# The sample tokens of a state-space layer: layout changes through a DRAM scratch instead of TensorE transposes

## The chip, the cores and the metric

One core of a Trainium2 chip runs the whole kernel. The time is device microseconds of one execution, lower is better; of the kernel before the median of three runs is given.

## The reference

One layer of a streaming encoder runs on 1024 prompt tokens and 64 sample tokens (a second group of requests with state from the past). Both share the weights, so the kernel puts them side by side: 1088 columns.

```
h = rmsnorm(x); proj = h @ w_in                      # 2048 -> 6152 columns
u, z_ssm, q, k, v, z_att, f = split(proj)
# S5 branch: 64 groups of 16 channels, a complex diagonal state of 64 per group
bb = coef * (u_group @ B)                            # per token
h_t = abar * h_(t-1) + bb_t                          # scan over tokens, sample tokens start from a given state
y = real(C h) + D * u
y_ssm = rmsnorm(gelu(y) * sigmoid(gelu(y) @ w_glu + b) * silu(z_ssm))
# attention branch with forget gates: softmax(q k / sqrt(d) + c_t - c_s) v, * silu(z_att), rmsnorm
out = x + concat(y_ssm, y_att) @ w_out
```

## The kernel before

**The GEMM that runs through.** Every projection is a sum of pieces. A piece is 256 rows of a weight (`PIECE` 2 tiles of 128) for 128 output columns. SP loads it into one of four `wraw` slots (`Weights.load`), ScalarE rounds it to `whi` (`split_hi`, L169), VectorE takes the rest `wlo` (`split_lo`, L173), and TensorE multiplies it in 18 matmuls (`multiply`, L185: three products, two row tiles, three column groups of 384, 384 and 320) into the three banks of `GB`. A load waits for the split of the piece four before it, and a cast for the multiplication four before it. So a load is issued about eight pieces before its own multiplication.

**State-space passes.** The 1024 state-space channels are worked in 8 passes j of 128 channels (8 groups of 16). A pass has 16 piece steps s: s = 0 to 7 multiply the u columns of the pass after, s = 8 to 15 the z columns of this one; u of pass 0 comes ahead of the loop, and the last pass has only steps 8 to 15. All the other work of the pass hangs on these steps by the tables `FULL` and `LAST`: each engine has its own program, and at step s it first does its part of the piece and then the state-space step that the table puts there. The order of each engine is thus written out by hand. In `FULL`:

- `first`, before s = 0: eight transposes into LS (L1030), copied out by ScalarE (L483) and VectorE (L699).
- `st1` at 0: the 128 channels of u are turned for each of the L = 8 phases of a block of 8 tokens. For the prompt (L1054) a transpose gives 128 blocks x 128 channels, for the sample (L1055) 8 blocks x 128 channels. They are copied to UC and UCS.
- `k` at 1; `st2` at 2: UC and UCS are turned back by group (L1072, L1074), which gives Ug, rows (phase, channel) and columns (block), with one column for the state at `NB` and the 8 sample blocks behind it.
- `s` at 3, `scan` at 4, `back` at 5, `h` at 7: the states, with VectorE and GpSimd. `y` at 9: 16 matmuls (L1093, L1094), copied to Y by ScalarE and VectorE (L536, L754).
- `yt` at 10 and `z` at 12: the same two layout changes backwards for y (L1008 and L1009, then L1016 and L1018). ScalarE takes the gelu of both parts (L464, L466) into U and stores U to `zg_s` (L469), `z_act` is counted, and TensorE's next `first` waits for it.
- `fin` at 13: the final states are stored. At 15 ScalarE waits for the store of U and writes Silu of z into U (L495), which frees the banks of `GB`.
- GpSimd prepares the tables for the next pass after `h` (G at L905 to L910, TR at L922 to L929). VectorE prepares Q at steps 13 and 14 (`prepare_q`, L663 to L672).
- `toeplitz` at 12 on SP: eight DMAs from the scratch `kpad_s` into MT (L364), between weight loads.

The attention phase follows, in 8 heads of 32 piece steps. Its first head carries, on each engine but SP, the last steps of the last pass (`tail`).

## Time and profile before

| | us |
|---|---|
| median of three runs | 2100.68 (2100.58 to 2102.3) |
| the profiled execution | 2099.1 |
| its span | 2097.4 |
| PE busy | 2023.6 (96%) |
| DVE busy | 1029.0 (49%) |
| ACT busy | 709.4 (34%) |
| POOL busy | 481.3 (23%) |

The span runs from the first to the last instruction; the rest of the execution's time lies around it. PE is TensorE, PEld its weight loads, DVE VectorE, ACT ScalarE, POOL GpSimd; SPq and ACTq are the queues that issue DMAs. In a row `x8` counts instructions and the idle time stands in brackets or behind the last bar, with what ended it. Matmuls are pipelined: one lasts longer in the trace than the slot it takes, so slots are read from the chain of waits or from differences of starts.

### The profile page before, as it was taken

To read this page: it belongs to the slowest core of one execution; us is meant where nothing else is said; L and a number is where in the kernel's file an instruction comes from. 1 tells how busy PE (TensorE), PEld (TensorE's weight loads), DVE (VectorE), ACT (ScalarE), POOL (GpSimd) and SP (SyncE) were. 2 spreads that over 40 slices of the span, in tenths; PEclk is the share of its full clock that TensorE was granted. 3 is DMA by queue.
4 is the path that set the end of the run, shared out by engine and by line. 5 is a ranking of instruction groups with operands and counts; after the bars stand their busy time and mean duration, and the time that the engine had idled before them with its cause. 6 is when DMAs were issued, how large, how long until landed. Compare 5 with 4: busy or idle time off the path is not lost.

```text
span 2097.4 us, 36580 instructions
## 1 busy us (share of the span) xinstructions
PE 2023.6 (96%) x12880; PEld 1952.5 (93%) x12880; DVE 1029.0 (49%) x2028; ACT 709.4 (34%) x1460; POOL 481.3 (23%) x748
## 2 busy tenths in 40 slices
PE   4899999999999999999999999999998999999997
PEld 3689999999999999999999999999998999999997
DVE  6465465555545354554635455463565553333332
ACT  6423333233342333343343334334355631111110
POOL 5764455444411001010010101001020112222222
PEclk8899999999999999999999999999999999999998
DMA  7222222222222213122131212112174433333331
GB/s 204 81 49 61 64 68 58 61 72 63 69 61 57 60 33 85 35 59 55 34 82 33 83 35 73 41 43 73 36 264 149 156 122 94 85 85 85 85 85 55
DMA packets 194713, 162.16 MB, mean 77 GB/s; under 512 B 26690, under 2 KB 176364, under 8 KB 193316
## 3 DMA queue, kind: packets, MB, share of 16 engines
q1 hardware_dynamic: 174224, 98.87, 18.1%
q0 software_dynamic: 14832, 51.26, 8.0%
q10 hardware_dynamic: 5604, 11.34, 1.5%
q8 instruction: 31, 0.51, 0.1%
q14 instruction: 22, 0.18, 0.0%
HBM read 124.47 MB, written 36.95 MB: 77 GB/s over the span
## 4 chain that ended last, share of the span: by engine, by line
PE 90%; DVE 4%; ACT 2%; issue 2%; DMA 1%; POOL 0%; ACTq 0%; DVEq 0%; SPq 0%; POOLq 0%
PE GB L185 64%; PE TB L185 9%; PE TB L1870 3%; PE TB L1891 3%; PE TB L1912 1%; PE TB L1084 1%; PE TB L1093 1%; PE TB L1094 1%; PE TB L1971 1%; PE TB L1931 1%; DVE XL L597 1%; DVE xt L589 0%; PE TB L970 0%; PE TB L1054 0%; PE TB L1856 0%
## 5 line engine op out<-in xcount | busy, mean ns | idle before, releaser
L185 PE MATMUL GB<-XH,whi 128*128 128x384 f32 (+1 forms) x2880 | 973.7, 338 | 6.3 <-ACT QR L1425 3.8
L185 PE MATMUL GB<-XH,wlo 128*128 128x384 f32 (+1 forms) x2880 | 943.1, 327 | 0.0
L185 PE MATMUL GB<-XL,whi 128*128 128x384 f32 (+1 forms) x2880 | 940.0, 326 | 0.0
L173 DVE TENSOR_TENSOR wlo<-wraw,whi 128x256 fp32r<-128x256 f32 x544 | 259.8, 478 | 738.5 <-ACT whi L169 734.2
L185 PEld LDWEIGHTS GB<-XH,whi 128*128 128x128 f32 x2880 | 541.5, 188 | 20.8 <-issue 14.8
L185 PEld LDWEIGHTS GB<-XL,whi 128*128 128x128 f32 x2880 | 542.1, 188 | 5.3 <-issue 3.8
L169 ACT CAST whi<-wraw 128x256 fp32r<-128x256 f32 x544 | 220.0, 405 | 954.6 <-PE GB L185 801.0
L185 PEld LDWEIGHTS GB<-XH,wlo 128*128 128x128 f32 x2880 | 541.0, 188 | 0.0
L1291 POOL DMA_DIRECT2D ya_s<-ZR x7 | 4.1, 586 | 729.5 <-DVE ZR L1655 729.5
L1702 DVE RECIPROCAL SQ<-SQ 128x136 f32<-128x136 f32 x128 | 127.5, 996 | 1.1
L185 PE MATMUL TB<-XH,wlo 128*128 128x384 f32 (+1 forms) x384 | 125.8, 328 | 0.0
L185 PE MATMUL TB<-XH,whi 128*128 128x384 f32 (+1 forms) x384 | 125.5, 327 | 0.0
L185 PE MATMUL TB<-XL,whi 128*128 128x384 f32 (+1 forms) x384 | 125.5, 327 | 0.0
L1474 ACT ACTIVATE PR<-PR,nmx 128x128 f32<-128x128 f32 (+8 forms) x72 | 53.4, 742 | 186.2 <-DVE nmx L1673 173.0
L1379 ACT ACT_TABLE_LOAD x64 | 82.1, 1283 | 1.2
L1870 PE MATMUL TB<-PT,VT 128*128 128x128 f32 x576 | 74.7, 275 | 0.8 <-ACT PT L1484 0.8
L1870 PEld LDWEIGHTS TB<-PT,VT 128*128 128x128 f32 x576 | 71.3, 191 | 1.5 <-ACT PT L1484 1.2
L1891 PE MATMUL TB<-KN,QN 128*128 128x512 f32 (+2 forms) x192 | 72.4, 486 | 0.0
L185 PEld LDWEIGHTS TB<-XH,whi 128*128 128x128 f32 x384 | 72.1, 188 | 0.1
L185 PEld LDWEIGHTS TB<-XH,wlo 128*128 128x128 f32 x384 | 72.1, 188 | 0.0
L185 PEld LDWEIGHTS TB<-XL,whi 128*128 128x128 f32 x384 | 72.0, 188 | 0.0
L1668 DVE CUSTOM_DVE_ANT_0 PR<-TB,NCB 128x128 f32<-128x128 f32 (+3 forms) x64 | 41.0, 640 | 33.3 <-PE TB L1891 22.2
(387 smaller groups left out, 2197.2 us busy)
## 6 DMA issues: line engine op xcount, KB each, us to landing
wraw<-in_w_in SPq DMA_DIRECT2D x384, 128.0 KB, 2.2
wraw<-in_w_out SPq DMA_DIRECT2D x128, 128.0 KB, 2.2
xt<-in_x_prompt SPq DMA_DIRECT2D x5, 1024.0 KB, 5.4
NCB<-nc_s POOLq DMA_DIRECT2D x8, 608.0 KB, 5.3
zg_s<-U ACTq DMA_DIRECT2D x8, 544.0 KB, 2.7
XL<-zg_s SPq DMA_DIRECT2D x8, 544.0 KB, 4.4
VR<-zg_s POOLq DMA_DIRECT2D x8, 544.0 KB, 6.3
KO<-zs_s POOLq DMA_DIRECT2D x8, 544.0 KB, 7.7
```

The source lines that it names most:

```text
L169: S.copy(whi[:, s % SPL], wraw[:, s % RAW]).then_inc(self.hi, 1)
L173: V.tensor_tensor(wlo[:, s % SPL], wraw[:, s % RAW], whi[:, s % SPL].bitcast(f32), ALU.subtract).then_inc(self.lo, 1)
L185: ins = T.matmul(group(GB if bank is None else bank, b), w[:, s % SPL, kk], x[:, k + kk, c:c + n], start=first and kk == 0 and i == 0, sto ...
L597: V.tensor_tensor(XL[:, 4 * b:4 * b + 4, m * P:m * P + n], tb, XH[:, 4 * b:4 * b + 4, m * P:m * P + n].bitcast(f32), ALU.subtract).then_in ...
L1084: ins = T.matmul(TB[g * NP:(g + 1) * NP, c:c + SC], LS[:, i, g * NP:(g + 1) * NP], Ug[:, 2 * (i % 4) + g], start=True, stop=True)
L1093: T.matmul(TB[:, c:c + SC], MT[:, g], Ug[:, g], start=True, stop=False)
L1379: o.then(S.activation(tabs[:], epsc[:], func))
L1474: S.activation(PR[0:n, 0:w], PR[0:n, 0:w], ACT.Exp, bias=nmx[0:n], accum_out=rsum[0:n]).then_inc(e["exp"], 1)
L1668: V.tensor_tensor_reduce(out=PR[0:n, 0:w - n], in0=TB[0:n, 0:w - n], in1=NCB[0:n, c:c + w - n], scale=1.0, scalar=-3e38, op0=ALU.add, op1= ...
L1702: o.then(V.reciprocal(a, a))
L1870: ins = T.matmul(O, VT[:, b], PT[:, b * P:(b + 1) * P], start=b == 0, stop=b == i)
L1891: ins = T.matmul(TB[:, c:c + cw], q, KN[:, c:c + cw], start=True, stop=True)
```

## The change

Of the 64 sample tokens, u and y no longer go through narrow transposes. For u, ScalarE writes the sample columns of the bank to UST (in phase order), SP stores UST to the scratch `us_s` (128 x 64 floats) and loads it back in eight DMAs, one for each phase, into USG; VectorE copies USG to its columns of Ug. For y, VectorE gathers the sample columns of Y into YSG, SP stores it to `vs_s` and loads it back in eight DMAs, one for each group, into YST; ScalarE takes the gelu from there, now at the step `fin` (13) and ahead of the stores of the final states, with the store to `zg_s` behind it (`zs_step`). Each load moves runs of 8 floats, 128 of them. SP's order is: u out at the end of a pass, u in after the load of step 0, y out after step 2 and y in after step 3 of the following pass. Pass 0 and the first head of the attention phase are written out on SP, and the last y goes into that head. The L1055, L1009, L1074 and L1018 transposes and the four UCS copies (L457, L509, L686, L713) are gone. The signals `dec_ready` and `g_neg` are dropped or counted on others.

```diff
+    us_s = scratch("us_s", [P, DEC])
+    vs_s = scratch("vs_s", [P, DEC])
...
-            UCS = sbp("UCS", [P, 1024])
+            UCS = sbp("UCS", [P, 576])
+            UST, USG, YSG, YST = (sbp(n, [P, DEC]) for n in ("UST", "USG", "YSG", "YST"))
...
 
+                SIO = 16 * (1 + L)
+
+                def sample_u_out(j, taken):
+
+                    sp.wait_ge(e["ga"], taken)
+                    sp.wait_ge(e["us_io"], SIO * j)
+                    sp.dma_start(us_s, UST[:]).then_inc(e["us_io"], 16)
+
+                def sample_u_in(j):
+
+                    sp.wait_ge(e["us_io"], SIO * j + 16)
+                    sp.wait_ge(e["st2_dve"], j)
+                    for r in range(L):
+                        sp.dma_start(USG[r * GC:(r + 1) * GC].rearrange("c (g n) -> c g n", g=8),
+                                     us_s.rearrange("(g c) (t n) -> t c g n", g=8, t=L)[L - 1 - r]).then_inc(e["us_io"], 16)
+
+                def sample_y_out(j):
+
+                    sp.wait_ge(e["y_dve"], 2 * (j + 1))
+                    sp.wait_ge(e["vs_io"], SIO * j)
+                    sp.dma_start(vs_s, YSG[:]).then_inc(e["vs_io"], 16)
+
+                def sample_y_in(j):
+
+                    sp.wait_ge(e["vs_io"], SIO * j + 16)
+                    sp.wait_ge(e["z_act"], j)
+                    for g in range(8):
+                        sp.dma_start(YST[g * GC:(g + 1) * GC].rearrange("c (t n) -> c t n", t=L),
+                                     vs_s.rearrange("(t c) (g n) -> g c t n", t=L, g=8)[g]).then_inc(e["vs_io"], 16)
+
...
                 for s in range(HP):
                     W.load(sp, s, s, 0, PIECE * s)
-                with sp.Fori(0, NJ - 1) as j:
+                def pass_of(j, y):
                     for s in range(NPC):
                         load(j, s)
+                        if not y and s == HP - 1:
+                            sample_u_out(0, 3)
+                        if s == (0 if y else HP):
+                            sample_u_in(j)
+                        if y and s == 2:
+                            sample_y_out(j - 1)
+                        if y and s == 3:
+                            sample_y_in(j - 1)
                         if s == FULL["toep"]:
                             toeplitz(j)
+                    sample_u_out(j + 1, 5 * j + 5)
+                pass_of(0, False)
+                with sp.Fori(1, NJ - 1) as j:
+                    pass_of(j, True)
                 for s in range(HP, NPC):
                     load(NJ - 1, s)
+                    if s == HP:
+                        sample_u_in(NJ - 1)
+                    if s == HP + 2:
+                        sample_y_out(NJ - 2)
+                    if s == HP + 3:
+                        sample_y_in(NJ - 2)
                 toeplitz(NJ - 1)
+
+                def tail(s):
+                    if s == 8:
+                        sample_y_out(NJ - 1)
+                    if s == 9:
+                        sample_y_in(NJ - 1)
+                return tail
...
-                    S.copy(cols(UZ, 2), group(GB, 2)).then_inc(e["ga"], count)
+                    S.copy(UZ[:, 2 * CW:SEQ], GB[:, 1024:1024 + SEQ - 2 * CW])
+                    act.wait_ge(e["us_io"], 16 * (1 + L) * u)
+                    S.copy(UST[:].rearrange("p (t n) -> p t n", t=L),
+                           GB[:, 1024 + SEQ - 2 * CW:1024 + TOK - 2 * CW].rearrange("p (n t) -> p t n", t=L)).then_inc(e["ga"], count)
 
                 def yt_step(j):
                     act.wait_ge(e["yt_mm"], j + 1)
                     S.copy(UC[:].rearrange("p (t g c) -> p g t c", t=L, g=8)[:, 0:4],
-                           TB[:, 512:1024].rearrange("p (g t c) -> p g t c", g=4, t=L))
-                    S.copy(UCS[0:8].rearrange("p (t g c) -> p g t c", t=L, g=8)[:, 0:4],
-                           TB[0:8, 3 * 512:4 * 512].rearrange("p (g t c) -> p g t c", g=4, t=L)).then_inc(e["yt_act"], 1)
+                           TB[:, 512:1024].rearrange("p (g t c) -> p g t c", g=4, t=L)).then_inc(e["yt_act"], 1)
+
+                zt = lambda a: a.rearrange("p (c t) -> p t c", t=L)
 
                 def z_step(j):
                     act.wait_ge(e["z_mm"], j + 1)
-                    zt = lambda a: a.rearrange("p (c t) -> p t c", t=L)
                     for hlf in range(2):
                         S.activation(zt(U[:, 0:SEQ])[:, 4 * hlf:4 * hlf + 4],
                                      TB[:, 512 * (1 + hlf):512 * (2 + hlf)].rearrange("p (t c) -> p t c", t=4), ACT.Gelu)
-                    S.activation(zt(U[:, SEQ:TOK]), TB[:, 0:DEC].rearrange("p (t c) -> p t c", t=L),
+
+                def zs_step(j):
+                    act.wait_ge(e["vs_io"], 16 * (1 + L) * (j + 1))
+                    S.activation(zt(U[:, SEQ:TOK]), YST[:].rearrange("p (t c) -> p t c", t=L),
                                  ACT.Gelu).then_inc(e["z_act"], 1)
                     act.wait_ge(e["z_act"], j + 1)
                     act.dma_start(zg_s[ds(j * P, P), :], U[:, 0:TOK]).then_inc(e["zg_out"], 16)
...
                         if s == at["z"]:
                             z_step(j)
                         if s == at["fin"]:
+                            zs_step(j)
                             fin_step(j)
                 for s in range(HP):
...
+                        zs_step(NJ - 1)
                         fin_step(NJ - 1)
                 return tail
...
                         if s == at["st2"]:
                             dve.wait_ge(e["st2_mm"], j + 1)
                             dve.wait_ge(e["zs_out"], 16 * j)
                             V.memset(Ug[:, :, NB:NB + 1], 0.0)
                             V.tensor_copy(Ug[:, 4:8, 0:NB], TB[:, 3 * 512:4 * 512].rearrange("p (g c) -> p g c", g=4))
-                            V.tensor_copy(Ug[:, :, NB + 1:SC], TB[:, 4 * 512:4 * 512 + DEC].rearrange("p (g c) -> p g c", g=8)
+                            dve.wait_ge(e["us_io"], 16 * (1 + L) * (j + 1))
+                            V.tensor_copy(Ug[:, :, NB + 1:SC], USG[:].rearrange("p (g c) -> p g c", g=8)
                                           ).then_inc(e["st2_dve"], 1)
                         if s == at["s"]:
...
+                            dve.wait_ge(e["y_act"], j + 1)
+                            dve.wait_ge(e["y_dve"], 2 * j + 1)
+                            dve.wait_ge(e["vs_io"], 16 * (1 + L) * j)
+                            V.tensor_copy(YSG[:].rearrange("p (g n) -> p g n", g=8), Y[:, :, NB + 1:SC]).then_inc(e["y_dve"], 1)
                         if s == at["yt"]:
                             yt_step(j)
...
                 gate(2)
                 def yt_step(j):
                     pe.wait_ge(e["y_act"], j + 1)
-                    pe.wait_ge(e["y_dve"], j + 1)
+                    pe.wait_ge(e["y_dve"], 2 * j + 1)
                     for g in range(8):
-                        T.transpose(TB[:, 512 + g * P:512 + (g + 1) * P], Y[:, g, 0:NB], ident[:])
-                        ins = T.transpose(TB[0:NBS, 3 * 512 + g * P:3 * 512 + (g + 1) * P], Y[:, g, NB + 1:SC], ident[:])
+                        ins = T.transpose(TB[:, 512 + g * P:512 + (g + 1) * P], Y[:, g, 0:NB], ident[:])
                     ins.then_inc(e["yt_mm"], 1)
 
                 def z_step(j):
                     pe.wait_ge(e["yt_act"], j + 1)
                     pe.wait_ge(e["yt_dve"], j + 1)
                     for t in range(L):
-                        T.transpose(TB[:, 512 + t * P:512 + (t + 1) * P], UC[:, t * P:(t + 1) * P], ident[:])
-                    for t in range(L):
-                        ins = T.transpose(TB[:, t * NBS:(t + 1) * NBS], UCS[0:NBS, t * P:(t + 1) * P],
-                                          ident[0:NBS, 0:NBS])
+                        ins = T.transpose(TB[:, 512 + t * P:512 + (t + 1) * P], UC[:, t * P:(t + 1) * P], ident[:])
                     ins.then_inc(e["z_mm"], 1)
...
                                 i = L - 1 - r
-                                T.transpose(TB[:, 3 * 512 + r * P:3 * 512 + (r + 1) * P], UZ[:, i:SEQ:L], ident[:])
-                                ins = T.transpose(TB[0:NBS, r * P:(r + 1) * P], UZ[:, SEQ + i:TOK:L], ident[:])
+                                ins = T.transpose(TB[:, 3 * 512 + r * P:3 * 512 + (r + 1) * P], UZ[:, i:SEQ:L], ident[:])
                             ins.then_inc(e["st1_mm"], 1)
...
                             for g in range(8):
-                                T.transpose(TB[:, 1024 + g * P:1024 + (g + 1) * P], UC[:, g * P:(g + 1) * P], ident[:])
-                            for g in range(8):
-                                ins = T.transpose(TB[:, 4 * 512 + g * NBS:4 * 512 + (g + 1) * NBS],
-                                                  UCS[0:NBS, g * P:(g + 1) * P], ident[0:NBS, 0:NBS])
+                                ins = T.transpose(TB[:, 1024 + g * P:1024 + (g + 1) * P], UC[:, g * P:(g + 1) * P], ident[:])
                             ins.then_inc(e["st2_mm"], 1)
                         if s == at["s"]:
...
-            def sync(sp):
-                with sp.Fori(0, NH) as h:
+            def sync(sp, state_space):
+                def head(h, s):
+                    col = h * P + 2 * D_SSM + D_ATT * (s // 8)
+                    W.load(sp, h * NPC + s, s, col, PIECE * (s % 8))
+                for s in range(NPC):
+                    head(0, s)
+                    state_space(s)
+                with sp.Fori(1, NH) as h:
                     for s in range(NPC):
-                        col = h * P + 2 * D_SSM + D_ATT * (s // 8)
-                        W.load(sp, h * NPC + s, s, col, PIECE * (s % 8))
+                        head(h, s)
...
```

## Rows read from the trace of the kernel before

**Rows 1.** The page: busy us (share of the span) xinstructions of each engine

```profile
PE 2023.6 (96%) x12880; PEld 1952.5 (93%) x12880; DVE 1029.0 (49%) x2028; ACT 709.4 (34%) x1460; POOL 481.3 (23%) x748
```

**Rows 2.** Waits of PE, whole span: total us, times, longest us

```profile
PE TB L1054 <- issue: 2.2, 8, 0.3
```

**Rows 3.** Chain of waits, 250 to 320 us: start us, us, engine, tile, line

```profile
284.92 0.11 PE TB L1009
...
293.37 0.59 PE TB L1018 x8
...
294.17 8.92 PE GB L185 x54
303.08 0.87 PE TB L1030 x8
...
306.94 0.29 issue
...
307.69 0.11 PE TB L1054
...
316.83 0.59 PE TB L1074 x8
```

**Rows 4.** PE by line, 115 to 605 us: busy us, mean ns, idle before

```profile
L1055 PE MATMUL TB<-ident,UZ 128*8 128x128 f32 x64 | 14.5, 274 | 0.0
```

**Rows 5.** Timeline of DVE, 245 to 320 us: start us, us, line and operation

```profile
281.87 0.59 DVE L754 COPY SS<-TB 128x411 f32<-128x411 f32 x1 [1.65 <-PE TB L1094]
...
297.60 0.42 DVE L173 TENSOR_TENSOR wlo<-wraw,whi 128x256 fp32r<-128x256 f32 x1 [3.02 <-ACT whi L169]
297.94 1.29 DVE L663 TENSOR_TENSOR UC<-PJ 128x576 f32<-128x576 f32 x1
...
300.36 2.27 DVE L666 TENSOR_TENSOR Q<-UC,UCS 64x576 f32<-64x576 f32 x2
302.75 0.43 DVE L173 TENSOR_TENSOR wlo<-wraw,whi 128x256 fp32r<-128x256 f32 x1
303.10 0.75 DVE L669 TENSOR_TENSOR UC<-PJ 128x576 f32<-128x576 f32 x1
...
306.45 0.68 DVE L699 COPY LS<-TB 128x512 f32<-128x512 f32 x1
```

**Rows 6.** Timeline of POOL, 283 to 305 us

```profile
296.42 0.62 POOL L922 TENSOR_TENSOR M<-TR,PJ 128x256 f32<-128x256 f32 x1
...
300.88 1.13 POOL L927 TENSOR_TENSOR TR<-M 128x256 f32<-128x256 f32 x1
302.18 0.56 POOL L929 COPY TR<-TR 128x72 f32<-128x72 f32 x1 [0.17 <-POOL TR L927]
```

**Rows 7.** Line 663, all passes: ns min/median/max, first and last start

```profile
L663 DVE TENSOR_TENSOR UC<-PJ x8: 759/1295/1295, 111.4 to 548.5; 128x576 f32<-128x576 f32 x8
```

**Rows 8.** Timeline of ACT, 265 to 335 us

```profile
297.16 0.41 ACT L169 CAST whi<-wraw 128x256 fp32r<-128x256 f32 x1 [0.87 <-PE GB L185]
...
302.25 1.30 ACT L495 ACTIVATE U<-GB 128x384 f32<-128x384 f32 x3 [0.19 <-ACT tabs L445]
...
305.66 0.59 ACT L483 COPY LS<-TB 128x512 f32<-128x512 f32 x1
```

**Rows 9.** SP: its timeline, and line 364 in all passes

```profile
267.02 3.69 SPq L364 DMA_DIRECT2D MT<-kpad_s  x8
...
290.58 0.37 SPq L164 DMA_DIRECT2D wraw<-in_w_in  x1
...
L364 SPq DMA_DIRECT2D MT<-kpad_s x64: 327/431/1534, 141.8 to 569.6; - x64
```

**Rows 10.** The page: DMA issues, KB each, median us from issue to landing

```profile
zg_s<-U ACTq DMA_DIRECT2D x8, 544.0 KB, 2.7
...
MT<-kpad_s SPq DMA_DIRECT2D x64, 64.0 KB, 2.5
...
CK<-in_cache_logf POOLq DMA_DIRECT2D x1, 4.0 KB, 2.3
```

More of the change, by code:

```diff
@@ L445, in table, with take_u @@
                     o.then(S.activation(tabs[:], epsc[:], func))
-                def take_u(tile, ready, count):
+                def take_u(u, tile, ready, count):
                     act.wait_ge(W.done[0], tile + 1)
@@ L507, in body @@
                             S.copy(UC[:].rearrange("p (g r c) -> p r g c", g=8, r=L)[:, 0:4],
[L508 to L510 removed]
+                                   TB[:, 3 * 512:4 * 512].rearrange("p (r g c) -> p r g c", r=4, g=8)).then_inc(e["st1_act"], 1)
                         if s == at["st2"]:
@@ L530, in body @@
                             act.wait_ge(e["ks_ready"], j + 1)
-                            act.wait_ge(e["dec_ready"], j + 1)
                             act.wait_ge(e["s_act"], 4 * j + 4)
@@ L648, in prepare @@
                     o.then(V.tensor_copy(DC[:], row(MG)[:, 0].unsqueeze(2).to_broadcast([P, 4, SC])))
-                    V.memset(DC[:, :, 0:NB + 1:NB], 0.0).then_inc(e["dec_ready"], 1)
+                    V.memset(DC[:, :, 0:NB + 1:NB], 0.0)
                     for i in range(2):
@@ L1143, in attention @@
                      "pt_mm", "pt_act", "pt_dve", "o_mm", "y", "v_mm", "v_act", "v_dve", "k_mm", "k_act", "k_dve",
-                     "in", "zs_in", "ys_out", "k_out", "v_out", "y_out", "ysq", "sqa", "init", "qg", "sqf", "sql", "or", "g_in", "g_a", "g_d", "g_t", "g_ev", "g_cum", "g_neg", "g_out")
+                     "in", "zs_in", "ys_out", "k_out", "v_out", "y_out", "ysq", "sqa", "init", "qg", "sqf", "sql", "or", "g_in", "g_a", "g_d", "g_t", "g_ev", "g_cum", "g_out")
             e = {n: sem("att_" + n) for n in names}
@@ L1280, in gpsimd @@
                 pool.dma_start(logf_sample[0, 0], lt[0:DEC, TT - 1]).then_inc(e["g_out"], 16)
-                pool.wait_ge(e["g_neg"], 2)
+                pool.wait_ge(e["g_cum"], 6)
                 pool.dma_start(nc_s[:, 0:SEQ], cum0).then_inc(e["g_out"], 16)
@@ L1593, in gates @@
                         V.tensor_tensor_scan(cum1, one8[:, 0:PAST + DEC], lfs, 0.0, ALU.mult, ALU.add).then_inc(e["g_cum"], 1)
-                        V.tensor_scalar(cum0, cum0, -1.0, None, ALU.mult).then_inc(e["g_neg"], 1)
+                        V.tensor_scalar(cum0, cum0, -1.0, None, ALU.mult).then_inc(e["g_cum"], 1)
                         dve.wait_ge(e["g_cum"], 4)
-                        V.tensor_scalar(cum1, cum1, -1.0, None, ALU.mult).then_inc(e["g_neg"], 1)
+                        V.tensor_scalar(cum1, cum1, -1.0, None, ALU.mult).then_inc(e["g_cum"], 1)
                 def add_squares(n):
@@ L2021, in _ @@
                     ring.move_on(0, 0)
-                    first[0](sp)
+                    rest = first[0](sp)
                     ring.move_on(128, 16)
-                    second[0](sp)
+                    second[0](sp, rest)
                 @block.scalar
```

17 lines of the change are left out of this document (5 added, 12 removed).

## The prediction

> **What bounds the kernel now.** The page first: TensorE is busy 96% of the span and VectorE 49% [rows 1]. So the question is which TensorE instructions go and what can newly make it wait. The waits of TensorE say how tight the fit is: in the state-space passes it waits once a pass, 0.3 us, just before line 1054 [rows 2]. Then the chain of waits through one pass [rows 3]: multiplication pieces (L185, 18 matmuls, 8.92 / 3 = 2.97 us each) and state-space steps follow each other on TensorE without a hole, except the 0.29 us at 306.94. The reader should see that every transpose in this chain costs its full time. The 0.29 us has an owner: the transposes at 307.23 need VectorE's copy of LS, which ends at 306.45 + 0.68 = 307.13 [rows 5]. VectorE's chain from the split at 297.60 to that copy is nearly back to back and just longer than TensorE's work beside it. Both matter below. All clock times are those of the profiled pass around 284 to 317 us.
>
> **What is removed.** Four groups of eight narrow transposes a pass: L1055 (u, 64 in all, so 8 in each of 8 passes) [rows 4], L1009 (y), L1074 (u again) and L1018 (y again). L1055 and L1009 are interleaved with wide ones; a slot in either group takes 0.11 us, wide or narrow (0.109 before rounding: eight wide ones take 0.87, as at 303.08) [rows 3]. That is 0.87 us for each group. L1018 and L1074 stand alone with 0.59 us each [rows 3]. Sum 0.87 + 0.87 + 0.59 + 0.59 = 2.92 us a pass, 8 x 2.92 = 23.4 us, all on the path. One doubt: L1055's narrow loads alternated with strided wide ones. If the wide ones alone need the slot of a matmul of 320 columns (a piece is 12 of 384 and 6 of 320 columns, so 2.97 / 17 = 0.175 and 0.146 us), 7 x 0.037 x 8 = 2 us of the gain would be missing. I take the 0.11, since the wide ones at 303.08 have it alone; 0 to 2 us stays in the range.
>
> The UCS copies on ScalarE and VectorE go with them. They hide beside multiplications today, none ends a wait that TensorE shows [rows 2], so I cost them at nothing.
>
> **What is added, and where it stands.** ScalarE: the take-over of u's last bank is cut into two copies, at most 0.59 us more, what 512 columns take at 305.66 [rows 8], before a bank that TensorE needs only after six matmuls in each of the two other banks, 2 x 1.0 us later: hidden. VectorE: one copy of 64 elements into YSG, which waits for ScalarE's y copy. Y is out of PSUM at 281.87 + 0.59 = 282.46 [rows 5]; TensorE's next step on it is the group around 284.92 [rows 3], so it is hidden too, and behind it on VectorE stands only the next split. Its u copy now reads USG instead of PSUM, same size.
>
> SP: per pass two stores and two groups of eight loads, 18 more issues. The nearest row is the MT load, eight issues from the same kind of scratch to 16 partitions with 128 runs: 3.69 us for eight, 0.43 median and 1.53 at most for one [rows 9]. Landing: 2.5 us for MT; 2.3 us for the row nearest in shape, cache_logf, 128 runs of 32 B; 2.7 us for the far larger zg store [rows 10]. Behind these issues in SP's queue stand the weight loads. A load issued at 290.58 follows the split four pieces before its own, so it has about four pieces, 12 us, less 2.2 us of landing, until ScalarE wants it, and three more pieces until TensorE does. The longest block is a store's landing plus eight issues, 2.7 + 3.7 = 6.4 us. It fits; today's MT group already blocks SP for 3.69 us unseen. I cost SP at 0 (bounds: 0 below; above, see the second rival). SP's unrolled first pass and first head add only instructions, 0; the merged signals (dec_ready gone, g_neg counted on g_cum) leave the same waits, 0.
>
> u has time: it is stored at the end of a pass and needed at piece 2 of the next, except in the first pass, where the loads follow a split at piece 0 by about 0.5 us, take 3.7 + 2.5 us, and are wanted two pieces and three transposing steps later, about 8.5 us. Hidden by 2 us.
>
> y is the tight one. The eight loads into YST stand behind the weight load at 290.58. The store stands one piece earlier, at 287.6 at the latest (290.58 - 2.97), and lands by 290.3. The eight issue from 290.95 to 294.6, the last lands about 294.2 + 2.5 = 296.7. ScalarE reads YST behind its cast at 297.16 + 0.41 [rows 8]. With L1009 and L1018 gone (0.87 + 0.59 = 1.46, of which only 0.59 falls after 290.58) that cast ends at 297.0. So ScalarE waits 0 to 0.7 us there. Then gelu 0.35, issue, zg landing 2.7 [rows 10]: 300.2 to 301.0, against the Silu that needs it at 302.25 - 0.59 = 301.7 [rows 8]. It holds. Queued behind the wait on ScalarE: the state stores, a cast with some 9 us of slack, the table and the Silu.
>
> **What is late next.** This I do not cost at nothing. GpSimd's preparation of TR starts behind VectorE's H work of the pass (not moved), and ends at 302.18 + 0.56 [rows 6]; VectorE's preparation of Q starts behind the split at 297.60, which TensorE's progress sets. Where they overlap both are slow: the first Q operation takes 0.76 us alone and 1.295 in the loop [rows 7], the TR operations 0.62 before 297.94 and 1.13 at 300.88 [rows 6]. After GpSimd is through, VectorE's same multiplication at 303.10 takes 0.75 [rows 5]. Counted in starts: four Q operations from 297.94 to 300.36 + 2.27 = 302.63 take 4.7 us against 4 x 0.75 alone, so each loses 0.43; a GpSimd one that is met loses about as much (0.4). TensorE reaches the split 1.46 us sooner against GpSimd's clock. Then six large TR operations instead of four lie beside Q, GpSimd ends at about 303.5, and the split at 302.75 - 1.46 and the multiplication at 303.10 - 1.46 fall under it as well, perhaps part of the next: 2 to 2.3 operations x 0.43 = 0.9 us. The chain that makes the 0.29 us hole has no other slack and the interval from the split to L1054 loses no TensorE work (three pieces and L1030), so the hole grows to 1.2 us, in the 7 passes that prepare a next one: 7 x 0.9 = 6.3 us. Bounds: 0 (GpSimd done in time) and 1.4 us (three operations and a longer one), 9.8 us. I take 0.9.
>
> The Trainium skill (SBUF — State Buffer, section "Who interferes with whom") says more sharply that a VectorE instruction with two SBUF inputs and a GpSimd one that reads SBUF exclude each other for a whole instruction. By that rule each of 2.3 operations would lose up to a whole 0.62 us instruction, 1.4 us a pass, which is the upper bound; the 0.43 from the rows stands in my sum.
>
> **Sum.** 2099.1 (the profiled execution: span 2097.4 and 1.7 around it) - 23.4 + 6.3 = 2082.0. The median before is 2100.68, 1.6 above that execution, so the forecast is 2083.6.
>
> **Rivals.** (1) No contention: GpSimd is not slowed and the hole stays 0.29. For it: GpSimd's end at 302.74 is 0.36 us before the next Q operation today, so it could just clear it if it ran ahead. Against: 1.46 is more than 0.36. Time 2100.7 - 23.4 = 2077.3; with the full lock instead, 2100.7 - 23.4 + 9.8 = 2087.1.
>
> (2) Slower: y comes back late. The place is ScalarE's wait before the YST gelu. With T the last landing, the Silu that frees the first bank starts at about T + 3.3 and ends 0.48 later; TensorE wants the bank at 303.96 - 1.46 = 302.5. So it costs from T = 298.7 on, one for one, and eats the gain from T = 302 (2.92 x 8 / 7 = 3.3 more): loads that take 11 us from 290.95 and not 5.8. With every issue at the 1.53 maximum and a landing of 3.5, T = 290.95 + 7 x 1.53 + 3.5 = 305.2: 6.5 us of bank wait and about 0.6 behind it for LS, minus the 0.3 hole, 7 x 6.8 = 48, 2100.7 - 23.4 + 48 = 2125. For it: short runs of 32 B, 1024 in a row, beside weight loads. Against: 0.43 median and the 2.3 us of 32 B runs. The Trainium skill (DMA: Bandwidth & Descriptors, "Specifications") puts full rate at 512 B and above and a read-modify-write below; the 2.3 us row says that this does not lengthen one such transfer.
>
> (3) No change: the same wait at about half that price, T near 302, 2097 to 2104.
>
> (4) SP starves the weights: needs a block beyond 10 us for ScalarE and 19 us for TensorE. It would show as waits before L185. I give it 1 in 100 and count it under (2).
>
> **Chances.** Forecast with holes of 0.6 to 1.2 us added, 0.62; no growth 0.16; the full lock 0.10; no change 0.04; slower 0.08. A measurement of this kernel tells 0.2%, 4.2 us, from no change. Faster 0.88, same 0.04, slower 0.08. The range takes the first three with the 2 us of doubt at either end: 2076 to 2091.
>
> **What would show it.** Right: L1009, L1018, L1055 and L1074 gone, TensorE's busy time about 23 us less in count of slots, a wait before L1054's successor of about 1.2 us instead of 0.3 in seven passes, with GpSimd's copy ending beside VectorE's second Q half; the SP queue waiting only for splits and its two stores. Wrong: a wait before the first bank of piece 0 whose releaser is ScalarE's Silu (rival 2), casts that wait for weight loads (4), or wide u transposes spaced by more than 0.11 us.

## The result and the profile after

| | us, median (lowest to highest) |
|---|---|
| before | 2100.77 (2100.58 to 2102.3) |
| changed | 2075.36 (2073.43 to 2078.09) |
| ratio | 0.9878, 95% interval 0.9861 to 0.9896 |
| forecast | 2083.6 (2076 to 2091) |

The changed kernel is 25.4 us faster; its profiled execution, at 2073.97 (span 2072.4), is 25.1 under that of before. The direction and the mechanism were as forecast. The size was not: 25.4 against 17.1, and the median lies 0.6 us below the range.

The page of the changed kernel, each engine's busy time, then its waits of TensorE (total us, times, longest us); they answer to [rows 1, 2]:

```profile
PE 1998.4 (96%) x12624; PEld 1932.8 (93%) x12624; DVE 1029.1 (50%) x2020; ACT 702.0 (34%) x1452; POOL 475.7 (23%) x748
```

```profile
PE TB L1113 <- issue: 4.2, 8, 0.6
```

256 transposes are gone (four groups of eight, eight passes). The hole at the wide u transposes (L1054 before, L1113 now) was 0.3 us and is 0.6, where 1.2 was forecast. No wait for the Silu, for a cast or for a weight load has come.

The chain of waits of the changed kernel through the same pass (start us, us, engine, tile, line; L187 is the multiplication, L1081, L1089, L1113 and L1130 answer to L1022, L1030, L1054 and L1072):

```profile
284.72 0.11 PE TB L1081
284.83 8.92 PE GB L187 x54
293.75 0.87 PE TB L1089 x8
...
297.61 0.58 issue
298.19 1.13 PE TB L1113 x8
...
306.05 0.88 PE TB L1130 x8
306.92 2.96 PE GB L187 x18
```

Two pieces of the chain of before, which the forecast did not look at, stand beside it:

```profile
293.96 0.21 PE TB L1022
...
317.42 3.17 PE GB L185 x18
```

The single transpose behind L1018 took 0.21 us; behind wide ones it takes 0.11 (L1081). The piece behind L1074 took 3.17 us; behind L1130 it takes 2.96. So the edge of a group of 8-row transposes had a price of its own in the work behind it: 0.10 us for one group, 0.21 us for the other. The 8-row transposes are not alone in this: the 16 short matmuls of the step `k` (L1063 before, L1121 now) are in both kernels, and the piece behind them takes 3.15 to 3.16 us in both.

### The profile page after: what moved, and what is told of

Its sections match the earlier page's. It is cut to its first block, busy times and chain, and to the rows that moved or that the text cites. A ratio compares the mean times of both kernels' runs of the same rounds, so it can differ in the third digit from the quotient of the medians.

```text
span 2072.4 us, 36133 instructions
## 1 busy us (share of the span) xinstructions
PE 1998.4 (96%) x12624; PEld 1932.8 (93%) x12624; DVE 1029.1 (50%) x2020; ACT 702.0 (34%) x1452; POOL 475.7 (23%) x748
## 4 chain that ended last, share of the span: by engine, by line
PE 89%; DVE 5%; ACT 2%; issue 2%; DMA 1%; POOL 0%; ACTq 0%; SPq 0%; DVEq 0%; POOLq 0%
PE GB L187 65%; PE TB L187 9%; PE TB L1930 3%; PE TB L1951 3%; PE TB L1972 1%; PE TB L1139 1%; PE TB L1148 1%; PE TB L1149 1%; PE TB L2031 1%; PE TB L1991 1%; DVE XL L659 1%; DVE xt L651 0%; PE TB L1916 0%; ACT L1439 0%; PE TB L1113 0%
## 5 line engine op out<-in xcount | busy, mean ns | idle before, releaser
L187 PE MATMUL GB<-XH,whi 128*128 128x384 f32 (+1 forms) x2880 | 974.2, 338 | 6.2 <-ACT QR L1485 3.8
L187 PE MATMUL GB<-XH,wlo 128*128 128x384 f32 (+1 forms) x2880 | 944.0, 328 | 0.0
L187 PE MATMUL GB<-XL,whi 128*128 128x384 f32 (+1 forms) x2880 | 940.8, 327 | 0.0
L187 PEld LDWEIGHTS GB<-XH,whi 128*128 128x128 f32 x2880 | 542.1, 188 | 20.3 <-issue 14.7
L187 PEld LDWEIGHTS GB<-XL,whi 128*128 128x128 f32 x2880 | 542.5, 188 | 5.3 <-issue 3.8
L187 PEld LDWEIGHTS GB<-XH,wlo 128*128 128x128 f32 x2880 | 541.5, 188 | 0.0
L187 PE MATMUL TB<-XH,wlo 128*128 128x384 f32 (+1 forms) x384 | 125.9, 328 | 0.0
L187 PE MATMUL TB<-XH,whi 128*128 128x384 f32 (+1 forms) x384 | 125.6, 327 | 0.0
L187 PE MATMUL TB<-XL,whi 128*128 128x384 f32 (+1 forms) x384 | 125.6, 327 | 0.0
L187 PEld LDWEIGHTS TB<-XH,whi 128*128 128x128 f32 x384 | 72.1, 188 | 0.1
L187 PEld LDWEIGHTS TB<-XH,wlo 128*128 128x128 f32 x384 | 72.2, 188 | 0.0
L187 PEld LDWEIGHTS TB<-XL,whi 128*128 128x128 f32 x384 | 72.1, 188 | 0.0
```

The lines of the kernel that those rows point to most:

```text
L187: ins = T.matmul(group(GB if bank is None else bank, b), w[:, s % SPL, kk], x[:, k + kk, c:c + n], start=first and kk == 0 and i == 0, sto ...
```

## The sum, term by term

The pass before this one starts its L1089 at this time in the changed kernel (chain of waits):

```profile
234.07 0.87 PE TB L1089 x8
```

From there to 293.75 is 59.68 us. Before, L1030 came at 303.08 [rows 3] and, one pass sooner, at 240.45, 62.63 us apart:

```profile
240.45 0.87 PE TB L1030 x8
```

| term, us a pass | forecast | measured |
|---|---|---|
| groups L1055, L1009, L1018, L1074 | −2.92 | −2.92 |
| what followed L1018 and L1074 | 0 | −0.31 |
| hole before the wide u transposes | +0.90 | +0.29 |
| sum | −2.02 | −2.94 (periods: −2.95) |

Over the kernel: 8 × 3.23 = 25.8 removed, 7 × 0.29 = 2.0 given back, 23.8 net. The forecast had 23.4 − 6.3 = 17.1. 1.3 of the 25.1 us are left over; 0.8 of them stand in a wait of the attention phase (PR: 5.4 us in all before, 4.6 now), not followed further, since four executions of the changed kernel spread over 4.7 us.

**Why the hole grew by 0.29 and not 0.9.** The timelines of VectorE and of GpSimd in the changed kernel (start us, us, engine, line, operation), answering to [rows 5, 6]:

```profile
278.56 0.44 DVE L710 COPY DC<-PJ 128x548 f32<-128x548 f32 x1
...
288.26 0.43 DVE L175 TENSOR_TENSOR wlo<-wraw,whi 128x256 fp32r<-128x256 f32 x1 [3.02 <-ACT whi L171]
...
293.30 0.76 DVE L175 TENSOR_TENSOR wlo<-wraw,whi 128x256 fp32r<-128x256 f32 x1
...
297.40 0.68 DVE L759 COPY LS<-TB 128x512 f32<-128x512 f32 x1
```

```profile
278.55 0.50 POOL L988 TENSOR_TENSOR M<-TR,PJ 128x8 f32<-128x8 f32 x1
...
287.78 0.62 POOL L985 TENSOR_TENSOR M<-TR,PJ 128x256 f32<-128x256 f32 x1
```

GpSimd's work behind H starts 7.76 us sooner than before, the split before Q 9.34 us (288.26 against 297.60): VectorE gained 1.58 us on GpSimd's start, about the 1.46 of the forecast. But GpSimd's first 256-column operation comes 8.64 us sooner (287.78 against 296.42), so it made up 0.88 us and only 0.70 of VectorE's gain was left. VectorE met what was expected in kind (the next split now takes 0.76 us and not 0.43), but less of it. In GpSimd's timeline of the kernel before, one of its small operations, normally 0.21 us, was caught under VectorE's copy to DC:

```profile
287.22 1.08 POOL L923 TENSOR_TENSOR M<-TR,PJ 128x16 f32<-128x16 f32 x1
```

In the changed kernel the same copy (L710) starts together with a GpSimd operation, which takes 0.50 instead of 0.20. That is 0.87 − 0.30 = 0.57 us of the 0.88 that GpSimd made up. In both kernels the operation ends some 0.07 us behind the copy to DC, so what counts is how long before that copy it started. The change moved this too: it dropped VectorE's copy to UCS (L686) between the copies to UC and to DC, which the forecast cost at nothing, and the copy to DC now starts 0.61 us behind the start of the one to UC and not 1.20. The experiments test the rest: that the overlap makes the hole (e6), that it can be moved away (e5), and that its size follows where GpSimd starts against VectorE (e7, and the table behind it).

**The way of y and u.** SP's timeline in this pass of the changed kernel, then line 390 in all passes (shortest/median/longest ns, first and last start), then ScalarE's timeline, answering to [rows 8, 9]:

```profile
282.58 3.65 SPq L390 DMA_DIRECT2D YST<-vs_s  x8
```

```profile
L390 SPq DMA_DIRECT2D YST<-vs_s x64: 332/430/438, 163.3 to 578.8; - x64
```

```profile
288.14 0.33 ACT L529 ACTIVATE U<-YST 128x64 f32<-128x64 f32 x1
```

The DMA issues of the changed kernel (KB each, median us from issue to landing), answering to [rows 10]:

```profile
YST<-vs_s SPq DMA_DIRECT2D x64, 4.0 KB, 1.7
```

Eight issues took 3.65 us (forecast 3.7), none more than 0.44; the landing, counted from the start of an issue, took 1.7 (forecast 2.5). The last of the eight issues, 0.43 us long, started at 282.58 + 3.65 − 0.43 = 285.8 and landed 1.6 us later, at 287.4. ScalarE's cast ended at 288.2, and the row of the gelu has no wait in brackets.

## The experiments

Ratios are against the kernel before, run on the same chip beside them.

**e1, e2, e3: one part alone.** e1 is the kernel before without the two groups of 8-row transposes, e2 without the two narrow groups of 128 rows; both leave out the sample part of u and y. e3 has the new way for u and the old one for y, and computes everything.

```
e1  -  ins = T.transpose(TB[:, t*NBS:(t+1)*NBS], UCS[0:NBS, t*P:(t+1)*P], ident[0:NBS, 0:NBS])      # and the same for u
e2  -  ins = T.transpose(TB[0:NBS, 3*512+g*P:3*512+(g+1)*P], Y[:, g, NB+1:SC], ident[:])            # and the same for u
e3  -  ins = T.transpose(TB[0:NBS, r*P:(r+1)*P], UZ[:, SEQ+i:TOK:L], ident[:])                      # and the 8-row group of u
    +  sample_u_out(j + 1, 5 * j + 5)                                                                # and sample_u_in, as in the change
```

> The kernel before, leaving out the two groups of 8-row transposes (L1018, L1074; the sample part of u and y is then not computed). Theory A, a change of the array's shape costs time after the group too: each group takes its 0.59 us, the piece behind L1074 falls from 3.17 to 2.96 us and the transpose behind L1018 from 0.21 to 0.11, 1.49 us a pass, 11.9 us; with at most 0.3 us more hole in 7 passes about 2090. Theory B, the group costs its slots alone (my prediction): 9.4 us, the following piece stays at 3.17, about 2092.

> The kernel before, leaving out the two groups of transposes with 8 columns out of 128 rows (L1055, L1009; sample part of u and y not computed). Theory A and B alike: 2 x 0.87 x 8 = 13.9 us, the wide transposes of u alone in slots of 0.11, the piece behind L1074 still 3.17. The hole before L1054 grows by 0 to 0.3 us a pass because TensorE reaches the split 0.87 us sooner. 2087 to 2089. If the strided wide ones need 0.146 alone: 2 us less gain.

> Only u goes through DRAM, y stays on narrow transposes. Neither u group lies between GpSimd's start after H and the split of step 13, so by the contention theory the hole stays at 0.29 us. Gain (0.87 + 0.59 + 0.21) x 8 = 13.4 us, 2087.3. If the hole grows for another reason (the DMAs, the dropped copies), it is seen here too: 0.58, 2089.4.

All three were slower, and by nearly the same: 2140.0 (ratio 1.0180, 1.0160 to 1.0199), 2136.91 (1.0172, 1.0155 to 1.0189) and 2136.09 (1.0167, 1.0150 to 1.0184) against 2098.87. No theory had that. The waits of TensorE in e1 name the place; then its timeline there, and one window (its length, then busy us and instructions of PE, PEld, DVE, ACT and POOL, granted clock, DMA share, GB/s):

```profile
PE GB L185 <- issue: 33.9, 6, 6.7
```

```profile
817.23 0.69 PE L185 MATMUL GB<-XH,whi 128*128 128x384 f32 x1 [5.59 <-issue]
```

```profile
820.00:823.00 3.00, 3.00 (x12) 3.00 (x11) 0.00 (x0) 0.00 (x0) 0.00 (x0) 0.50 0.00 0
```

The wait stands where the loop of the attention phase jumps back, six times, and is released by nothing that the profile shows. Behind the one shown, the granted clock is 0.50, the 1.2 GHz level, for a whole piece, which takes 5.81 us (from 817.23) where 2.97 is usual; from 823 on it is back at 2.4 GHz. Other jumps cost less: the time from the first matmul of the attention scores (KN by QN) in front of a jump to the first one behind it is 42.83 us at all six jumps of e9, which lacks the wait, and 49.4 to 52.0 in e1. The six together cost 48.3 us, wait and low clock, of the 2140.0 − 2090.5 = 49.5 between the two. The queue table of the page (packets, MB, share of the engines' time) says what TensorE waited for, first e1, then the changed kernel:

```profile
q8 instruction: 85, 1.39, 0.3%
```

```profile
q8 instruction: 31, 0.51, 0.1%
```

Each packet is 16 KB. The trace has the time of each one. In the kernel before none comes between 811.5 and 1556.9 us, while the loop repeats. In e1 nine come in every round, 54 in all: four around the jump (805.8, 810.3, 815.0 and 819.2 us, beside the wait from 811.6 to 817.2) and five spread over the 120 us behind it. So the instructions of the loop are loaded anew in each round. All kernels have the same loop; what differs is where it starts in TensorE's instructions. The next batches rest on that.

**e8, e9, e10: the same parts, with the loop back at its old place.** e8 is e3, e9 is e1 and e10 is e2, and each adds 64 counted no-wait instructions on TensorE ahead of the loop.

```
        for m in range(TT):
            tiles(m)
+           for _ in range(16 if m in (1, 2, 3, 4) else 0):
+               stand(pe, "pe")
```

> e3 (u through DRAM, y on TensorE) with 64 semaphore increments added to TensorE's program ahead of the state-space passes, while it waits for x. They put the attention loop back at instruction 3426 of TensorE's program, where the kernel before has it (e1 to e3: 3362; a matmul counted as two). Theory, code position: the six waits of 5.6 us at the loop's wrap and the 54 extra instruction packets are gone, and the gain shows: (0.87 + 0.59 + 0.21) x 8 = 13.4 us, hole as before at 0.29: ratio 0.9936. Rival, the waits come from what was taken out: 2136 again.

> e1 (8-row transposes left out, the sample part of u and y not computed) with the same 64 increments. Code position: as in e1's own expectation, theory A 11.9 us less than before, less up to 0.3 x 7 for the hole: 10 to 12 us; theory B 9.4 less the hole. Otherwise 2140 again.

> e2 (the transposes with 8 columns left out, sample part not computed) with the same 64 increments. Code position: 13.9 us less, minus the growth of the hole (0 to 0.3 x 7): 12 to 14 us less. Otherwise 2137 again.

The loss of 37 to 41 us is gone: 2089.36 (0.9947, 0.9934 to 0.9960), 2090.47 (0.9954, 0.9941 to 0.9967) and 2089.29 (0.9955, 0.9942 to 0.9969), 31 instruction packets each. The chains of waits give the price of each group. First e9, without 8-row groups; then e10, with them and without the 128-row ones; then e8:

```profile
178.40 0.87 PE TB L1029 x8
...
182.25 0.46 issue
...
192.28 2.96 PE GB L185 x18
...
239.64 0.87 PE TB L1029 x8
```

```profile
175.44 0.87 PE TB L1031 x8
...
179.87 1.13 PE TB L1055 x8
...
188.61 0.59 PE TB L1074 x8
189.20 3.17 PE GB L185 x18
...
236.60 0.87 PE TB L1031 x8
```

```profile
178.16 0.87 PE TB L1079 x8
...
239.10 0.87 PE TB L1079 x8
```

The piece behind the 8-row group is 3.17 us in e10 and 2.96 in e9: the 0.21 us belong to that group. Periods: e9 61.24, 1.39 less than 62.63; 2 × 0.59 + 0.31 = 1.49, less 0.17 by which its hole grew (0.46), is 1.32. (In the middle passes of e9 the hole is 0.58 and the period 61.37 to 61.42.) e10 61.16, 1.47 less: 2 × 0.87, less 0.29 by which its hole grew (0.58), is 1.45. e8 60.94, 1.69 less: 0.87 + 0.59 + 0.21 = 1.67, its hole 0.29 as before. The wide u transposes alone take 1.13 us in e10, 0.35 for the first behind a hole and 0.11 for each of seven, so their stride costs nothing: the doubt of 2 us in the forecast is answered with 0.

**e11: the changed kernel with the same 64 instructions.** It keeps all the work and moves only the loop's start.

> The changed kernel, correct, with 64 semaphore increments on TensorE ahead of the passes: the attention loop moves from instruction 3298 to 3362, where e1 to e3 had it. Code position: six waits of 5.6 us at the wrap, 54 extra instruction packets, about 2075 + 40 = 2115. Rival (the DMA route or the removal protects it): 2075 to 2077.

2126.33 (1.0130, 1.0115 to 1.0144) against 2099.09, 85 instruction packets. Its waits of TensorE:

```profile
PE GB L187 <- issue: 31.6, 6, 6.3
...
PE TB L1115 <- issue: 6.8, 8, 0.9
```

By the distance across a jump (49.3 to 51.1 us for 42.83) the six jumps cost 44.6 us, of 51 measured against the changed kernel; the holes take 7 × 0.37 = 2.6 more, and the rest was not followed. The state-space work is the same instruction for instruction, and yet the hole is 0.94 us and not 0.58. Two of GpSimd's small operations met splits on the way (0.52 us instead of 0.24, and 0.49 instead of 0.29), so GpSimd reached its large operations about 0.4 us later against VectorE. The hole grew here by 0.65 against the kernel before, not far from the 0.9 of the forecast; in the kernel as changed it did not.

**e12: the kernel before with 192 such instructions.** If one packet holds 256 instructions (an assumption that no run measures) and the place decides by its remainder to 256, this must be slow too, since before, at 64 more, it is at the remainder of e1.

```
-               for _ in range(16 if m in (1, 2, 3, 4) else 0):
+               for _ in range(48 if m in (1, 2, 3, 4) else 0):
```

> The kernel before, whole and correct, with 192 semaphore increments on TensorE ahead of the passes: the attention loop moves from instruction 3426 to 3618 = 3362 + 256. If only the place within a block of 256 instructions counts (the instruction packets are 16 KB, 256 instructions of 64 B): six waits of 5.6 us at the wrap, 85 packets and more, 2099 + 40 = 2139. If the absolute place or the removal counts: 2099.

2157.61 (1.0278, 1.0261 to 1.0295) against 2100.66, 86 packets, waits of TensorE:

```profile
PE GB L185 <- issue: 33.0, 6, 5.9
...
PE TB L970 <- issue: 9.2, 2, 5.2
```

The jumps cost 47.3 us by the distance across them. Most of the rest of the 57.0 us stands ahead of the passes, at waits like that of L970, where the added instructions stand: the first transposes into LS start at 120.4 us instead of 111.4. Starts of the loop, counted in TensorE's instructions of the program, a matmul as two:

| kernels | loop starts at | remainder to 256 | instruction packets |
|---|---|---|---|
| before, e8, e9, e10 | 3426 | 98 | 31 |
| changed, e4 to e7, e13 to e15 | 3298 | 226 | 31 |
| e1, e2, e3, e11 | 3362 | 34 | 85 |
| e12 | 3618 | 34 | 86 |

The two slow rows share a remainder and not a place. More remainders were not tried. The count is that of the program, 1484 instructions for a round of the loop, where the trace shows some 1590 (750 matmuls, as many weight loads and 90 others). So the differences between the rows (−128, −64 and +192 against before) are firm, and the remainders themselves less so.

**e4 to e7: what makes the hole.** e4 is the changed kernel again. e5 issues VectorE's two halves of Q one step sooner each; e6 cuts GpSimd's last, 256-column level of TR down to 16 columns, which leaves the tables of all passes but the first incomplete; e7 adds an idle copy of 512 columns on VectorE ahead of its copy into UC in the step of y.

```
e5  -  prep=10, qa=13, qb=14
    +  prep=10, qa=12, qb=13
e6  +  if lv == NLV - 1 and not isinstance(j, int):
    +      n = 4
e7  +  V.tensor_copy(YX[0:8], TB[0:8, 1024:1536])
```

> The changed kernel again, beside the next three on one chip. 2075 within 2 us.

> The changed kernel with VectorE's two halves of Q at steps 12 and 13 instead of 13 and 14. Theory: the hole before the wide transposes of u is VectorE's chain from the split of step 13 through Q to the copy of LS. Moved 3 us forward, the chain has slack: hole 0 in 7 passes, 0.58 x 7 = 4.1 us less than the changed kernel. Rival: something else (ScalarE's LS copy behind Silu and the table load, ready at 297.1 against a piece that ends at 297.6) sets the hole at 0.1 to 0.3 us: 2 to 3 us less. Second rival: Q meets more of GpSimd and delays the split of step 13, as TensorE waits before pieces: slower than the changed kernel.

> The changed kernel, in which GpSimd does the last level of TR on 4 columns instead of 64 for every pass but the first (the tables of later passes are then stale). Contention theory: no large GpSimd operation lies beside Q, the four first Q operations take 0.75 each, VectorE's chain is about 2 us shorter and the hole is 0; 4.1 us less than the changed kernel. Rival, the hole is VectorE's own work: it stays at 0.58.

> The changed kernel with one idle copy of 8 x 512 put back on VectorE at step 10, so that the copy to DC starts 0.6 us later, as far behind the y step as before. Theory: the hole grew by only 0.29 and not 0.9 us because the copy to DC now blocks GpSimd for 0.3 us (0.50 against 0.20) and not for 0.9 (1.08 against 0.22). With the delay GpSimd is blocked for about 0.9 us again, its last level starts 0.6 us later against the split, and the hole grows from 0.58 to 0.8 to 1.2: 2 to 4 us slower than the changed kernel. Rival, the position of the copy to DC doesn't matter: no change.

| | us | ratio | hole, us |
|---|---|---|---|
| e4 | 2076.70 | 0.9888 (0.9871 to 0.9904) | 0.58 |
| e5 | 2072.17 | 0.9864 (0.9848 to 0.9881) | 0 |
| e6 | 2071.03 | 0.9863 (0.9845 to 0.9881) | 0 |
| e7 | 2078.43 | 0.9895 (0.9878 to 0.9911) | 0.93 |

VectorE's timeline of e6, then of e7, with GpSimd's operation that falls on the same time in e7:

```profile
289.09 0.77 DVE L725 TENSOR_TENSOR UC<-PJ 128x576 f32<-128x576 f32 x1
```

```profile
289.10 0.78 DVE L175 TENSOR_TENSOR wlo<-wraw,whi 128x256 fp32r<-128x256 f32 x1 [3.02 <-ACT whi L171]
```

```profile
288.98 0.62 POOL L987 TENSOR_TENSOR M<-TR,PJ 128x256 f32<-128x256 f32 x1
```

With GpSimd's large operations gone, the Q operations take 0.77 us each, not 1.17 to 1.29 as in the changed kernel, and the hole is gone. In e7 the split itself is met (0.78 instead of 0.43) and the hole is 0.93. So GpSimd's large operations beside Q make the hole, and where they start decides its size. In e5 TensorE waits at this place only in the first pass, and the wide u group costs less as well, as its chain of waits shows:

```profile
235.64 0.87 PE TB L1089 x8
...
239.50 0.88 PE TB L1113 x8
```

0.88 us instead of 1.13: the first transpose takes 0.35 after a hole and 0.11 without one. A hole of 0.58 us therefore costs 0.83. e5 computes everything, and it is the best version of those that do: 4.5 us under e4 by the medians, 5.7 by the profiled executions, where 7 × 0.83 = 5.8 is expected.

e7's edit cost 1.7 us by the medians, where 2 to 4 were expected; 7 × 0.35 = 2.5 us stand in its holes. It did so by a later start of GpSimd's large operations. No single small operation was caught for 0.9 us: the copy to DC held two of them (0.40 and 0.46 us for 0.20), and two more met splits (0.42 for 0.24, 0.48 for 0.30).

**One number orders the holes.** Take by how much VectorE's split before Q starts behind GpSimd's first 256-column operation of TR: 297.60 − 296.42 = 1.18 us before, 288.26 − 287.78 = 0.48 in the changed kernel. Read in the same way in each pass behind the first, in all kernels in which both chains are whole and nothing later ends the hole:

| kernels and passes | lead of GpSimd over the split, us | hole, us |
|---|---|---|
| e3, e12 (five passes of seven in each) | 1.58 | 0.10 to 0.12 |
| before, e8, the other passes of e3 and e12 | 1.18 | 0.29 |
| e1 (six passes), e9 (three) | 0.88 | 0.46 |
| e2, e10 | 0.55 | 0.58 |
| changed, e4, the other passes of e1 and e9 | 0.48 | 0.58 |
| e7 | 0.12 | 0.93 |
| e11 | 0.11 | 0.94 |

The hole follows the lead, whichever edit set it. The lead itself moves from one pass to the next even in one kernel, and there the meeting at the copy to DC is what differs: in e9 the small GpSimd operation takes 0.81 us in the three passes with a lead of 0.88 and 1.09 in the four with 0.48; in e3 and e12 it takes 0.81 in the passes with 1.58 and 1.09 in those with 1.18. So 0.28 us there are worth 0.40 us of lead and 0.12 to 0.19 us of hole.

**e13, e14: y comes back one or two pieces later.** The second rival of the forecast had a point from which it decides; here it is moved past it.

```
e13  -  if y and s == 3:           e14  -  if y and s == 3:
     +  if y and s == 4:                +  if y and s == 5:
```

> The changed kernel, correct, with the eight loads of y one step later on SP (after the load of step 4). My second rival put the price at: none up to a last landing at 298.7, then one for one. The landing moves by 2.98 us, from 287.5 to 290.5 on the changed kernel's clock, 0.7 us past ScalarE's point 288.2 plus the slack of 1.6 us that the zg store has before Silu (293.25): 0.7 to 1.2 us a pass, 5 to 8 us slower than the changed kernel. If y has more slack than that: no change.

> The same with the loads two steps later: the landing at 293.5, 3.0 us more a pass than e13, so 26 to 29 us slower than the changed kernel: slower or equal to the kernel before (2101 to 2105). If ScalarE's wait is covered elsewhere, less.

2083.91 (0.9923, 0.9906 to 0.9939) and 2124.67 (1.0121, 1.0101 to 1.0141) against 2100.66. The changed kernel, not run again with them, had 2075.36 and 2076.70. Waits of TensorE, e13 and then e14:

```profile
PE GB L187 <- ACT U L558: 10.3, 7, 1.8
```

```profile
PE GB L187 <- ACT U L558: 28.9, 7, 4.3
...
PE TB L1089 <- ACT U L529: 6.9, 7, 1.1
```

It is the forecast's place: the Silu that frees the first bank. In e13 the last of y lands at 292.26 in the pass shown and the bank comes at 297.96, 5.70 us later. Its chain of waits (DMA is the landing, L503 the table load), and TensorE's timeline:

```profile
290.65 1.61 DMA YST<-vs_s
...
295.74 1.28 ACT L503
```

```profile
297.96 0.45 PE L187 MATMUL GB<-XH,whi 128*128 128x384 f32 x1 [1.38 <-ACT U L558]
```

The forecast had 3.8 us (3.3 to the Silu's start and 0.48). It had seen the state stores and the cast queued behind the gelu and still reckoned them to lie beside the zg transfer; they go from 292.80 to 295.72 and the table load ends at 297.02, so ScalarE's own queue is what is late, not the transfer. So the point of decision lies 1.9 us sooner than forecast. In the changed kernel y lands at 287.4 and the bank is wanted at 294.62: 7.2 − 5.7 = 1.5 us to spare.

e13 lost 7.2 to 8.6 us against the changed kernel; 5 to 8 were expected. e14 lost 48 to 49 instead of 26 to 29. One part of the difference is the clock: behind the wait the first piece takes up to twice its time. The chain of waits, then the window (columns as above):

```profile
246.03 5.81 PE GB L187 x18
```

```profile
246.00:251.80 5.80, 5.77 (x19) 5.73 (x20) 2.16 (x4) 2.85 (x5) 0.00 (x0) 0.50 0.38 125
```

2.98 is usual; in the next pass it is 4.88. Over the seven passes it is three times near the larger and four times near the smaller, 3 × 2.83 + 4 × 1.90 = 16.1 us. 28.9 + 6.9 + 16.1, less the holes of 4 us that are gone, is 48.

**e15: three times the loads of u**, the second and third set into buffers that nobody reads.

```
-  for r in range(L):
+  for i in range(3 * L):
```

> The changed kernel, correct, with u's eight loads issued three times (the extra two into unused buffers): SP is held 2.1 + 24 x 0.46 = 13 us instead of 5.7 once a pass. My slack: 12 us less 2.2 until ScalarE wants the load, 9 us more until TensorE does. So ScalarE's cast waits some 2 us once a pass, TensorE not at all: the same as the changed kernel within 2 us. If SP was near its limit: a wait before a piece of 3 us or more a pass, over 20 us slower.

2080.42 (0.9905, 0.9889 to 0.9922) against 2100.66, 4 to 5 us more than the changed kernel; 0 to 2 were expected. The largest new wait of TensorE:

```profile
PE TB L1142 <- DVE U L782: 3.8, 1, 3.8
```

It stands in the first pass, where the forecast gave u 2 us of margin. In the others the longer queue pushed y: ScalarE waited for YST in all seven passes (6.5 us in all, 1.2 at most) and TensorE in five of them for the Silu (1.5 in all), in part instead of the old hole. Sixteen more issues a pass on SP, 7.5 us of queue time, made no cast or split wait for a weight load.

## Why the forecast was wrong in size

- **What is bound, and where.** Right. TensorE is busy 96% before and after, and every removed transpose was paid for in full: 2.92 us a pass, narrow or wide.
- **The removed sum (23.4).** Mis-sized: 25.8. The term stopped at the groups' own time. The 8-row groups also lengthened the work behind them by 0.10 and 0.21 us (e9 against e10; e8 for u alone). The signs were there in the trace of before: 3.17 for a piece where 2.97 is usual, and 0.21 for a transpose where 0.11 is.
- **The hole before the wide u transposes (6.3).** Mis-sized: 2.0. Cause and place were right (e5, e6), the bounds (0 to 9.8) held it. The failed step is the one from "VectorE reaches the split 1.46 us sooner" to "two more operations are met": it left GpSimd's clock as it was. From the end of H, which comes 7.76 us sooner, GpSimd made up 0.88 us, 0.57 of it because VectorE's copy to DC caught it less hard, with the UCS copy ahead of it gone (a copy that the forecast cost at nothing). Its lead over the split therefore fell from 1.18 to 0.48 us, and not to 1.18 − 1.46 = −0.28, where no run lies. The price for a given lead was about right: where the lead fell by 1.07 (e11) the hole grew by 0.65, and at the forecast's rate of 0.9 for 1.46 that is 0.66. A chain in which each half shifts the other can't be moved by a constant; e7 and e11 have holes of 0.93 and 0.94 for nearly the same work.
- **The way of y.** Right in result, off in two sizes that nearly cancel: y landed 7.2 us ahead of the wanted bank instead of 302.5 − 296.7 = 5.8 (0.8 of the difference by the shorter landing), and the point of decision lies 1.9 us sooner (e13). The margin was 1.5 us and not 2. That rival's price for late loads (2125 for 6.5 us of lateness) left out the clock: e14 has 2124.67 for waits of 5.1 us a pass, so the two times agree by chance.
- **The way of u, SP, the copies, the signals.** Nothing on TensorE's own path, as costed (what the dropped UCS copy did to the hole stands above); e8's period has no term left for them, and e15 shows SP's slack for weight loads, with a margin of the first pass that 7.5 us more of queue use up.
- **The wide u transposes' stride.** 0 of 0 to 2 us (e10).
- **Chances.** The result lies beyond "no growth" (2077.3), which had 0.16, though the hole did grow: the 2.4 us of the edges, which no case held, outweigh the 2.0 of the hole.
- **Not in any case.** The place of the attention loop in TensorE's instructions. Removing 128 of them moved it from remainder 98 to 226, both good. With 64 less, e1 to e3, the same kind of gain turned into a loss of 37 to 41 us. The forecast was spared that by luck, and no row of the kernel before would have told it.

## What to carry to other kernels

Price a removed group by the period of the loop or by its neighbours' lengths beside the usual ones, not by its own time alone; the excess behind it goes too. Where the next bound is the overlap of two engines that slow each other, read how far one engine leads the other where they meet, give the term its bounds, since small meetings on the way shift that lead, and try to move the work apart by a step (e5: 4.5 us for two numbers). When a change that only removes work makes the kernel slower, look at the waits with no releaser and at the packets of the instruction queue before you look for a cause in the work.

## What was not expected of the hardware

- The start of a loop of some 1500 TensorE instructions decides whether a round costs 6.5 to 9.2 us at the jump and nine 16 KB packets (e1, e11, e12), or nothing: slow at two starts with remainder 34 of the program's count, free at 98 and 226. What in the remainder decides stays open, as only three were seen.
- After waits of 4.1 us (e14) and 5.59 us (e1) TensorE's granted clock is at 0.50, the 1.2 GHz level, for up to one piece (5.81 us instead of 2.97). After the 1.38 us of e13 the granted clock was 1.00 and the piece took 3.1 us.
- Eight-row transposes take 0.074 us each (0.59 for eight) but lengthen what follows by 0.10 to 0.21 us a group (e9 against e10), and the first transpose after a hole takes 0.35 us instead of 0.11 (e5 against the changed kernel).
- Small overlaps of VectorE and GpSimd add up. One GpSimd operation of 0.21 us lasts 0.81 or 1.09 us at VectorE's copy to DC, and the 0.28 us between the two change the hole two steps later by 0.12 to 0.19 us (e9, e3, e12).
- Loads with runs of 32 B in DRAM, 4 KB each, landed 1.7 us after their issue, sooner than the 64 KB loads of MT (2.5) [rows 10].
